# Dilated attention heads of a hybrid decoder layer: the middle statistics travel by DMA through DRAM, and the second stage runs 14 units behind

## The chip, the core and the metric

One core of a Trainium2 chip runs the whole layer in one launch. The metric is the device time of that core in microseconds, the median of three runs.

## The reference, cut to what matters

One input projection gives queries, keys, values and gates for three groups of heads: A (6 heads, banded, with a sink per head), B (6 heads, dilated) and C (4 heads, cross attention to 256 memory tokens). The outputs are gated, joined, projected, normalised and added to the input. The change is about B, where every head is computed three times, with strides 1, 4 and 16, and the three results are weighted by their softmax denominators:

```python
B_CONFIGS = ((128, 1), (512, 4), (2048, 16))
...
        for (win, dil) in B_CONFIGS:
            qs = to_strided(qb * scale, dil)[:, :, :, None, :]
            o, lse = banded_attention(qs, to_strided(kb, dil), to_strided(vb, dil),
                                      win // dil, None)
            outs.append(from_strided(o[:, :, :, 0], B, dil).astype(jnp.float32))
            lses.append(from_strided(lse[..., 0], B, dil))
        wts = jax.nn.softmax(jnp.stack(lses, axis=0), axis=0)
        ob = jnp.sum(wts[..., None] * jnp.stack(outs, axis=0), axis=0)
```

## The kernel before, in words

Three stages follow each other: the projection (to about 1045 us of the profiled execution), attention (to about 1770 us), and the output projection. The change touches attention alone.

**Units, pairs, phases.** Attention of a head runs over two halves of the sequence, so B has 12 phases (head, half), and so has A; C has 8. A unit is 128 queries against 128 or 256 keys. A phase of B has 48 units in 24 pairs: 16 far units (stride 16, pairs 0 to 7), then 8 middle units (stride 4, pairs 8 to 11), 8 near units (stride 1, pairs 12 to 15), 8 middle units (16 to 19) and 8 near units (20 to 23). The first half's far units have 128 keys, the second half's 256. A phase of A has 8 pairs.

**Two stages per pair.** The first stage: TensorE multiplies queries and keys into one of three PSUM places (`scores`, L1311 to L1355), VectorE adds the mask, takes the row's extreme value and writes to SBUF (L1455), ScalarE takes the exponential and its row sum (L1621). The second stage: VectorE multiplies by the unit's weight (`scale`, L1544), TensorE transposes (L1424), ScalarE copies the transpose to SBUF (L1645, L1648), TensorE multiplies with the values (L1408) into one of two banks; VectorE and ScalarE empty a bank after its last pair (L1575, L1609, L1658).

**The exchange.** A row of a far unit, of a middle unit and of a near unit stands for three different tokens, so before the weights can be computed the extremes and sums of the far and the middle units must be brought to the rows of the near units, and the weights must be brought back. Both ways go over TensorE: VectorE spreads 16 far columns with a 0/1 matrix into `moved` (L1489, L1523), TensorE multiplies that by a fixed matrix (L1362, L1369); for the middle ones TensorE multiplies by four fixed 128 x 128 matrices, `group4` (L1364 there, L1371 back), and VectorE picks the right quarter and sums (L1494, L1497 there, L1528, L1532 back). Between the two, VectorE and ScalarE do some small operations on 16 to 48 columns (L1501 to L1519, L1634). The result `coef` is what `scale` waits for.

**The order of the work** is written out by hand, in rounds and slots. A round of B has 24 slots. In slot i each engine handles pair i of the first stage of the newest phase (a), one pair of the second stage of an older phase (c or b), and pieces of the exchange of phase c, the one before a. `TAIL` says how many slots the second stage of a phase starts after the round of its first stage ended: 18. In the round after its first stage, a phase has its exchange in slots 1 to 14: VectorE L1489 at slot 1, TensorE L1362 and L1364 at slot 4, VectorE at slots 5 and 6, ScalarE L1634 at slot 7, VectorE at 9 and 10, TensorE L1369 and L1371 at slot 13, VectorE L1528 to L1532 at slot 14. VectorE scales three slots ahead of the transposes, so from slot 15. Where B gives way to A, the first round of A has 24 slots and the second 22; in the first 11 slots of each there is only second-stage work of B, and A's 8 pairs are spread over the rest:

```python
            lag = (b or c).g.TAIL
            keep = c.g.TAIL if a else 0
            n = lag + c.g.NP - keep
```

**Queues.** SyncE issues all loads and stores of attention in one written order, each behind waits on counters of the first or the second stage. GpSimd's queue issues nothing while B runs: its last DMAs of the projection stage load the first keys and the constants (L984 to L990, among them `sel`, which holds `group4`), and its next one waits for the tenth phase of A (L1919). The fourth PSUM place of the scores, `ps_x`, is the exchange's while B runs; A uses it for scores, so A's fourth pair waits for B's last `coef_ready` (L1344). In A, VectorE copies the head's two sink values to `sink_now` at the first slot of each phase and waits for its own copy (L1447 to L1449).

## Time and profile before

| | before |
|---|---|
| runs, us | 2152.70, 2151.43, 2144.21 |
| median | 2151.43 |
| profiled execution, own time | 2152.24 |
| its span | 2150.1 |
| mean granted TensorE clock | 0.973 |
| busy share of the span: TensorE, VectorE, ScalarE, GpSimd | 95%, 73%, 63%, 5% |

The span goes from the first to the last instruction of the profiled execution; its own time is 2.1 us longer, and 0.8 us above the median. Busy shares are over the whole span, in which B's attention is about a fifth; what limits B must be read in its own stretch. TensorE's busy time is modelled and includes matmuls in flight.

### The profile page before, as it was taken

How to read it: one execution, taken by the hardware profiler on the slowest of the kernel's cores; microseconds unless marked ns; L12 is line 12 of the kernel's file. 1: busy time of each engine (PE TensorE's matmuls, PEld its weight loads, DVE VectorE, ACT ScalarE, POOL GpSimd, SP SyncE). 2: the span in 40 equal slices, each digit the busy share in tenths (PEclk: the TensorE clock that was granted, in tenths of full speed). 3: DMA queues.
4: the chain of work that ended last, by engine and by line, in shares of the span. 5: the costliest groups of instructions: out<-in, count | busy, mean ns of one | idle time of the engine just before them, and what ended most of it. 6: DMA issues, size and time to landing. Idle time of an engine off the chain costs nothing. (4 is left out here: it accounts for less than half of the span.)

```text
span 2150.1 us, 39340 instructions
## 1 busy us (share of the span) xinstructions
PE 2040.4 (95%) x12892; PEld 1717.2 (80%) x12892; DVE 1559.2 (73%) x4410; ACT 1352.9 (63%) x3520; POOL 115.9 (5%) x116
## 2 busy tenths in 40 slices
PE   5999999999999999999889999999999998899998
PEld 4787778888888888888778888887888887688886
DVE  6564674546654574436589999989799997888886
ACT  7454454544555464343699999989699997533333
POOL 1232310000000000002100000000000000000000
PEclk7999999999999999999889999999999999999999
DMA  4466576777577667588876687686779895345543
GB/s 158 152 229 222 177 242 180 217 247 217 155 223 212 225 196 235 184 286 272 201 148 138 130 167 143 131 161 139 150 184 220 227 249 171 98 164 168 176 160 113
DMA packets 351736, 401.40 MB, mean 187 GB/s; under 512 B 105616, under 2 KB 255248, under 8 KB 346688
## 3 DMA queue, kind: packets, MB, share of 16 engines
q1 hardware_dynamic: 343120, 364.80, 62.0%
q0 software_dynamic: 8432, 34.30, 5.2%
q8 instruction: 97, 1.59, 0.3%
q14 instruction: 87, 0.71, 0.1%
HBM read 255.62 MB, written 143.39 MB: 186 GB/s over the span
## 5 line engine op out<-in xcount | busy, mean ns | idle before, releaser
L854 PE MATMUL p_ps<-p_u_hi,p_w_hi 128*128 128x512 f32 x1344 | 534.0, 397 | 26.7 <-DVE p_p_c L739 10.8
L856 PE MATMUL p_ps<-p_u_hi,p_w_lo 128*128 128x512 f32 x1344 | 526.6, 392 | 0.0
L855 PE MATMUL p_ps<-p_u_lo,p_w_hi 128*128 128x512 f32 x1344 | 525.6, 391 | 0.0
L570 DVE TENSOR_TENSOR p_w_lo<-p_w_raw,p_w_hi 128x512 fp32r<-128x512 f32 x336 | 246.6, 734 | 327.0 <-ACT p_w_hi L423 325.4
L1621 ACT ACTIVATE probs<-probs,a_stat 128x256 f32<-128x256 f32 (+1 forms) x896 | 437.4, 497 | 38.9 <-DVE a_stat L1455 36.5
L423 ACT ACTIVATE p_w_hi<-p_w_raw 128x512 fp32r<-128x512 f32 x336 | 211.2, 629 | 329.0 <-PE p_ps L856 304.7
L854 PEld LDWEIGHTS p_ps<-p_u_hi,p_w_hi 128*128 128x128 f32 x1344 | 254.2, 189 | 85.4 <-issue 13.0
L856 PEld LDWEIGHTS p_ps<-p_u_hi,p_w_lo 128*128 128x128 f32 x1344 | 253.7, 189 | 54.4
L855 PEld LDWEIGHTS p_ps<-p_u_lo,p_w_hi 128*128 128x128 f32 x1344 | 254.2, 189 | 50.8
L1455 DVE CUSTOM_DVE_ANT_0 probs<-a_ps_s,fixed 128x256 f32<-128x256 f32 (+1 forms) x704 | 251.9, 398 | 48.3 <-PE a_ps_s L1354 45.7
L1424 PE MATMUL a_ps_t<-fixed,probs 128*128 128x128 f32 x1660 | 262.0, 279 | 23.6 <-ACT a_pT L1645 16.5
L1544 DVE TENSOR_SCALAR probs<-probs,a_coef 128x256 f32<-128x256 f32 (+1 forms) x896 | 264.5, 341 | 3.0
L1645 ACT ACTIVATE a_pT<-a_ps_t 128x512 f32<-128x512 f32 (+1 forms) x412 | 232.8, 568 | 20.7 <-PE a_ps_t L1424 20.6
L1408 PE MATMUL a_ps_o<-a_pT,a_v 128*64 128x128 f32 x3320 | 238.4, 283 | 0.0
L1353 PE MATMUL a_ps_s<-k_hi,q 128*128 128x256 f32 (+1 forms) x672 | 216.4, 341 | 15.4 <-PEq L266 5.8
L1424 PEld LDWEIGHTS a_ps_t<-fixed,probs 128*128 128x128 f32 x1660 | 194.8, 143 | 39.5 <-DVE probs L1544 23.3
L1408 PEld LDWEIGHTS a_ps_o<-a_pT,a_v 128*64 128x64 f32 x3320 | 183.4, 138 | 36.8 <-issue 34.4
L1354 PE MATMUL a_ps_s<-k_lo,q 128*128 128x256 f32 (+1 forms) x672 | 191.1, 301 | 0.0
L1621 ACT ACTIVATION_READ_ACCUMULATOR probs<-probs,a_stat 128x1 f32 x896 | 182.0, 203 | 0.0
L1353 PEld LDWEIGHTS a_ps_s<-k_hi,q 128*128 128x128 f32 x672 | 136.6, 203 | 44.7 <-issue 32.8
L2225 PE MATMUL f_ps<-f_w_hi,parts_hi 128*128 128x512 f32 x368 | 144.4, 392 | 6.5 <-DVE probs L2141 4.1
L2226 PE MATMUL f_ps<-f_w_lo,parts_hi 128*128 128x512 f32 x384 | 150.1, 391 | 0.0
(202 smaller groups left out, 2762.6 us busy)
## 6 DMA issues: line engine op xcount, KB each, us to landing
p_w_raw<-in_w_in SPq DMA_DIRECT2D x156, 256.0 KB, 3.7
p_w_raw<-scratch_w_s SPq DMA_DIRECT2D x144, 256.0 KB, 3.6
scratch_qk_hi<-p_out_a SPq DMA_DIRECT2D x80, 256.0 KB, 4.0
scratch_qk_lo<-p_out_b SPq DMA_DIRECT2D x80, 256.0 KB, 4.1
a_v<-scratch_v SPq DMA_DIRECT2D x40, 512.0 KB, 8.2
scratch_gate<-p_out_a SPq DMA_DIRECT2D x64, 256.0 KB, 3.8
scratch_v<-p_out_a SPq DMA_DIRECT2D x256, 64.0 KB, 2.3
a_gate<-scratch_gate SPq DMA_DIRECT2D x64, 256.0 KB, 6.0
```

Source lines behind the costliest of these rows:

```text
L423: nc.scalar.activation(w_hi[:, m % 3, :, :], w_raw[:, entry(j, g), :, :], ACT.Copy).then_inc(w_hi_ready, 1)
L570: nc.vector.tensor_tensor(w_lo[:, m % 3, :, :], w_raw[:, entry(j, g), :, :], w_hi[:, m % 3, :, :].bitcast(F32), ALU.subtract).then_inc(w_l ...
L854: nc.tensor.matmul(bank, hi, u_hi[j][:, k, :], start=j < 2 and k == 0, stop=False, skip_group_check=True)
L855: nc.tensor.matmul(bank, hi, u_lo[j][:, k, :], start=False, stop=False, skip_group_check=True)
L856: last = nc.tensor.matmul(bank, lo, u_hi[j][:, k, :], start=False, stop=k == KH - 1, skip_group_check=True)
L1353: nc.tensor.matmul(out, w, keys_of(keys_hi, u), start=True, stop=False)
L1408: last = nc.tensor.matmul(place_of(ps_o[j * HD:(j + 1) * HD, bank % 2, :], u), v[name][:, half, tile, :], pT[:, e % 4, j, at * P:(at + 1) ...
L1424: last = nc.tensor.transpose(ps_t[:, e % 2, j, at * P:(at + 1) * P], probs[:, s, 2 * e + j, at * P:(at + 1) * P], ident[:])
L1455: last = nc.vector.tensor_tensor_reduce(out=probs[:, s, 2 * slot + j, a:], in0=ps_s[:, slot % NS, j, a:], in1=masks[u.kind][:, a:], scale= ...
L1544: last = nc.vector.tensor_scalar(place, place, coef[:, s, u.column:u.column + 1], None, ALU.mult)
L1621: last = nc.scalar.activation(place, place, ACT.Exp, scale=-1.0, bias=stat[:, s, 0, u.column:u.column + 1], accum_out=stat[:, s, 1, u.colu ...
L1645: nc.scalar.activation(pT[:, e % 4, :, a[0]:], ps_t[:, e % 2, :, a[0]:], ACT.Copy).then_inc(turned_copied, 1)
```

## The change

The way of the middle statistics and weights is taken from TensorE and VectorE and given to DMAs on GpSimd's queue. When 20 of the 24 pairs of a phase have their sums, GpSimd stores 32 columns of `stat` to a DRAM scratch, waits, and issues four loads that bring them back in the new arrangement; VectorE waits for them at slot 2 of the next round. When the weights are ready (slot 5), GpSimd stores 16 columns, waits and issues four loads into `coef`; VectorE waits for them before pair 8's `scale`. `group4`, `picked` and the picking operations go; three operations on two of the groups at once become two operations each. The far statistics are spread at slot 9 of the phase's own round, right after their pairs, and multiplied at slot 11; the far weights at slots 5 and 7. The other operations of the exchange move to slots 1 to 9, at three places inside a slot, with other work between dependent ones. `TAIL` becomes 14. In A the copy of the sinks goes, and the operands are read from the table itself.

```diff
-    TAIL = 18 if kind == "B" else 4
+    TAIL = 14 if kind == "B" else 4
...
-        def exchange(phase, slot):
-            p, s = number(phase), phase[1]
-            if kind == "B" and slot == 4:
-                pe.wait_ge(spread, p + 1)
+        def gather(phase, slot):
+            if kind == "B" and slot == 11:
+                pe.wait_ge(spread, number(phase) + 1)
                 for x in range(2):
-                    nc.tensor.matmul(ps_x[:, 16 * x:16 * x + 16], moved[:, x, :], col16, start=True, stop=True)
-                for b in range(NCH):
-                    last = nc.tensor.matmul(ps_x[:, 128 + 32 * b:160 + 32 * b].rearrange("p (x n) -> p x n", x=2), group4[:, b, :],
-                                            stat[:, s, :, 16:32], start=True, stop=True)
+                    last = nc.tensor.matmul(ps_x[:, 16 * x:16 * x + 16], moved[:, x, :], col16, start=True, stop=True)
                 last.then_inc(gathered, 1)
-            if kind == "B" and slot == 13:
-                pe.wait_ge(spread_back, p + 1)
-                nc.tensor.matmul(ps_x[:, 64:80], moved[:, 2, :], col16, start=True, stop=True)
-                for r in range(NCH):
-                    last = nc.tensor.matmul(ps_x[:, 256 + 16 * r:272 + 16 * r], group4[:, r, :], work[:, 7, 16:32],
-                                            start=True, stop=True)
-                last.then_inc(gathered_back, 1)
+
+        def give_back(phase, slot):
+            if kind == "B" and slot == 7:
+                pe.wait_ge(spread_back, number(phase) + 1)
+                nc.tensor.matmul(ps_x[:, 64:80], moved[:, 2, :], col16, start=True, stop=True).then_inc(gathered_back, 1)
...
-            if kind == "A" and slot == 0:
-                dve.nop(nofuse=True)
-                nc.vector.tensor_copy(sink_now[:, s, :], sink[:, :, bass.ds(h, 1)].rearrange(
-                    "p a o -> p (a o)")).then_inc(sink_ready, 1)
-                dve.wait_ge(sink_ready, p + 1)
-                start = sink_now[:, s, 1:2] if kind == "A" else 3e38
+                start = sink[:, 1, h:h + 1] if kind == "A" else 3e38
...
-        def inverse(phase, slot):
+        def inverse(phase, slot, place):
 
             p, s = number(phase), phase[1]
-            if slot == 1:
+            if (slot, place) == (1, 0):
                 dve.wait_ge(sums_ready, p * NP + NP)
                 if kind == "A":
                     dve.wait_ge(exps_ready, p + 1)
-                    nc.vector.tensor_tensor(work[:, 1, :], work[:, 0, :], stat[:, s, 1, :],
-                                            ALU.add).then_inc(step, 1)
+                    nc.vector.tensor_tensor(work[:, 1, :], work[:, 0, :], near_stat(s, 1), ALU.add).then_inc(step, 1)
                     dve.wait_ge(step, p + 1)
-                    nc.vector.reciprocal(coef[:, s, :], work[:, 1, :]).then_inc(coef_ready, 1)
-                else:
-                    nc.vector.reciprocal(coef[:, s, :], stat[:, s, 1, :]).then_inc(coef_ready, 1)
-
-        def exchange(phase, slot):
+                nc.vector.reciprocal(coef[:, s, :], work[:, 1, :] if kind == "A" else near_stat(s, 1)).then_inc(coef_ready, 1)
+
...
+        def exchange(phase, slot, place):
...
-            if slot == 1:
+            at = (slot, place)
+            done = p * DVE_STEPS
+            far = ps_x[:, 0:32].rearrange("p (x b) -> p x b", x=2)
+            middle = middles.rearrange("p (b x c) -> p x c b", x=2, c=NCH)
+            by_chunk = lambda of: of.rearrange("p (c b) -> p c b", b=NCH)
+            low, ex, inv = work[:, 1, 0:16], work[:, 3, :], work[:, 6, 0:16]
+            if at == (1, 2):
+                dve.wait_ge(max_ready, p * NP + NP)
+                dve.wait_ge(gathered, p + 1)
+                nc.vector.tensor_tensor(work[:, 0, 0:16], far[:, 0, :], near_stat(s, 0), ALU.min).then_inc(step, 1)
+            if at == (2, 0):
+                dve.wait_ge(step, done + 1)
+                dve.wait_ge(middle_loaded, 64 * p + 64)
+                nc.vector.tensor_tensor(by_chunk(low), middle[:, 0, :, :], by_chunk(work[:, 0, 0:16]), ALU.min).then_inc(step, 1)
+            if at == (2, 1):
+                dve.wait_ge(step, done + 2)
+                nc.vector.tensor_tensor(work[:, 2, 0:16], low, far[:, 0, :], ALU.subtract)
+                nc.vector.tensor_tensor(by_chunk(work[:, 2, 16:32]), by_chunk(low), middle[:, 0, :, :], ALU.subtract)
+                nc.vector.tensor_tensor(work[:, 2, 32:48], low, near_stat(s, 0), ALU.subtract).then_inc(shifted, 1)
+            if at == (4, 0):
+                dve.wait_ge(exps_ready, p + 1)
                 dve.wait_ge(sums_ready, p * NP + NP)
-                nc.vector.tensor_tensor(moved[:, 0:2, :].rearrange("p x (r a) -> p x r a", a=8),
-                                        stat[:, s, :, 0:16].unsqueeze(3).broadcast_to([P, 2, 16, 8]),
-                                        sel16.unsqueeze(1).unsqueeze(1).broadcast_to([P, 2, 16, 8]), ALU.mult).then_inc(spread, 1)
...
+                nc.vector.tensor_tensor(work[:, 4, 0:16], ex[:, 0:16], far[:, 1, :], ALU.mult)
+                nc.vector.tensor_tensor(by_chunk(work[:, 4, 16:32]), by_chunk(ex[:, 16:32]), middle[:, 1, :, :], ALU.mult)
+                nc.vector.tensor_tensor(work[:, 4, 32:48], ex[:, 32:48], near_stat(s, 1), ALU.mult).then_inc(step, 1)
+            if at == (4, 1):
+                dve.wait_ge(step, done + 3)
+                nc.vector.reduce_sum(work[:, 5, 0:16], work[:, 4, :].rearrange("p (a n) -> p n a", a=3),
+                                     mybir.AxisListType.X).then_inc(step, 1)
+            if at == (4, 2):
+                dve.wait_ge(step, done + 4)
+                nc.vector.reciprocal(inv, work[:, 5, 0:16]).then_inc(step, 1)
+            if at == (5, 0):
+                dve.wait_ge(step, done + 5)
+                nc.vector.tensor_tensor(work[:, 7, 0:16], ex[:, 0:16], inv, ALU.mult)
+                nc.vector.tensor_tensor(work[:, 7, 16:32].rearrange("p (b c) -> p c b", c=NCH), by_chunk(ex[:, 16:32]),
+                                        by_chunk(inv), ALU.mult).then_inc(weights_ready, 1)
...
+            if at == (5, 1):
+                dve.wait_ge(weights_ready, p + 1)
                 nc.vector.tensor_tensor(moved[:, 2, :].rearrange("p (n a) -> p n a", a=8),
                                         work[:, 7, 0:16].unsqueeze(2).broadcast_to([P, 16, 8]),
                                         sel16.unsqueeze(1).broadcast_to([P, 16, 8]), ALU.mult).then_inc(spread_back, 1)
-            if slot == 14:
+            if at == (9, 0):
                 dve.wait_ge(gathered_back, p + 1)
-                own(nc.vector.tensor_tensor(picked[:, 0:64].rearrange("p (n b) -> p n b", b=NCH),
-                                            ps_x[:, 256:320].rearrange("p (n b) -> p n b", b=NCH),
-                                            col4.unsqueeze(1).broadcast_to([P, 16, NCH]), ALU.mult))
-                nc.vector.tensor_copy(coef[:, s, 0:16], ps_x[:, 64:80])
-                nc.vector.reduce_sum(coef[:, s, 16:32].rearrange("p (c r) -> p r c", r=NCH),
-                                     picked[:, 0:64].rearrange("p (r c b) -> p r c b", r=NCH, b=NCH),
-                                     mybir.AxisListType.X).then_inc(coef_ready, 1)
+                nc.vector.tensor_copy(coef[:, s, 0:16], ps_x[:, 64:80]).then_inc(coef_ready, 1)
...
+        def spread_far(phase, slot):
+
+            if kind != "B" or slot != 9:
+                return
+            p, s = number(phase), phase[1]
+            dve.wait_ge(sums_ready, p * NP + 8)
+            nc.vector.tensor_tensor(moved[:, 0:2, :].rearrange("p x (r a) -> p x r a", a=8),
+                                    stat[:, s, 0:32].rearrange("p (x r) -> p x r", x=2).unsqueeze(3).broadcast_to([P, 2, 16, 8]),
+                                    sel16.unsqueeze(1).unsqueeze(1).broadcast_to([P, 2, 16, 8]), ALU.mult).then_inc(spread, 1)
...
                 dve.wait_ge(coef_ready, p + 1 + C1)
+            if kind == "B" and e == 8:
+                dve.wait_ge(middle_back, 64 * p + 64)
...
-            if kind == "B" and slot == 7:
-                act.wait_ge(shifted, 2 * p + 1)
+                nc.scalar.activation(work[:, 0, :], near_stat(s, 0), ACT.Exp,
+                                     bias=sink[:, 0, phase[0]:phase[0] + 1]).then_inc(exps_ready, 1)
+            if kind == "B" and slot == 3:
+                act.wait_ge(shifted, p + 1)
                 nc.scalar.activation(work[:, 3, :], work[:, 2, :], ACT.Exp).then_inc(exps_ready, 1)
...
+    def pool_parts(pool):
+
+        def gather(phase):
+
+            p, s = number(phase), phase[1]
+            pool.wait_ge(sums_ready, p * NP + 20)
+            pool.dma_start(sc["middle_stats"], stat[:, s, 32:64]).then_inc(middle_stored, 16)
+            pool.wait_ge(middle_stored, 32 * p + 16)
+            for b in range(NCH):
+                pool.dma_start(middles[:, 8 * b:8 * b + 8],
+                               sc["middle_stats"][32 * b:32 * b + 32, :].rearrange("j (r e) -> r j e", r=NCH)).then_inc(middle_loaded, 16)
+
+        def give_back(phase):
+
+            p, s = number(phase), phase[1]
+            pool.wait_ge(weights_ready, p + 1)
+            pool.dma_start(sc["middle_weights"], work[:, 7, 16:32]).then_inc(middle_stored, 16)
+            pool.wait_ge(middle_stored, 32 * p + 32)
+            for r in range(NCH):
+                pool.dma_start(coef[:, s, 16 + 4 * r:20 + 4 * r],
+                               sc["middle_weights"][32 * r:32 * r + 32, :].rearrange("j (b c) -> b j c", c=NCH)).then_inc(middle_back, 16)
+        return named(gather=gather, give_back=give_back)
...
-                    c.parts.exchange(c.phase, i)
+                    c.parts.give_back(c.phase, i)
+                for v in slot.new:
+                    a.parts.gather(a.phase, v)
                 if slot.two_before and slot.two_before[1] % 2:
                     for x, e in (slot.three_before, slot.two_before):
                         x.parts.times_values(x.phase, e)
...
-                if c and c.g.kind != "B":
-                    c.parts.exchange(c.phase, i)
+                if c:
+                    c.parts.exchange(c.phase, i, 0)
                 if slot.ahead:
                     x, e = slot.ahead
                     x.parts.scale(x.phase, e)
+                if c:
+                    c.parts.exchange(c.phase, i, 1)
                 for v in slot.new:
                     a.parts.scores(a.phase, v)
...
-                if c and c.g.kind == "B":
-                    c.parts.exchange(c.phase, i)
+                if c:
+                    c.parts.exchange(c.phase, i, 2)
+                for v in slot.new:
+                    a.parts.spread_far(a.phase, v)
...
+        def pool_round(a, c, b, d):
+            if c and c.g.kind == "B":
+                c.parts.give_back(c.phase)
+            if a and a.g.kind == "B":
+                a.parts.gather(a.phase)
...
+                rounds(pool, pool_round, lambda g: g.pool_parts(pool))
...
+        "middle_stats": scratch("middle_stats", [P, 32]), "middle_weights": scratch("middle_weights", [P, 16]),
...
-    sel = np.concatenate([j % 8 == n(8), j // 8 == n(16), j // 32 == n(4)]
-                         + [j == 32 * b + n(P) % 32 for b in range(NCH)], 1).astype(np.float32)
+    sel = np.concatenate([j % 8 == n(8), j // 8 == n(16)], 1).astype(np.float32)
```

## Rows read from the trace of the kernel before

**Rows 1.** Windows: three of B's ten full rounds and the sum of all ten; busy us, clock, DMA share

```profile
1139.78:1179.56 39.78, 37.07 (x367) 32.25 (x366) 37.37 (x176) 37.15 (x127) 0.00 (x0) 1.00 0.80 154
...
1258.77:1299.85 41.08, 41.08 (x389) 36.70 (x390) 36.81 (x178) 37.46 (x134) 0.00 (x0) 0.94 0.69 135
...
1339.64:1378.97 39.33, 38.70 (x386) 34.34 (x385) 36.68 (x176) 36.78 (x134) 0.00 (x0) 1.00 0.69 140
...
sum 399.70, PE 383.35 PEld 337.04 DVE 370.44 ACT 371.31 POOL 0.00; mean PE 38.33 PEld 33.70 DVE 37.04 ACT 37.13 POOL 0.00
```

**Rows 2.** Waits in the ten full rounds, 1100.04 to 1499.74: total, times, longest

```profile
ACT probs L1621 <- DVE a_stat L1455: 22.4, 45, 0.9
DVE probs L1455 <- PE a_ps_s L1354: 21.6, 43, 1.7
PE a_ps_t L1424 <- ACT a_pT L1645: 11.1, 25, 1.8
...
ACT a_pT L1645 <- PE a_ps_t L1424: 4.7, 10, 0.6
```

**Rows 3.** TensorE's middle exchange: its instructions, and the way back in the timeline

```profile
L1364 PE MATMUL a_ps_s<-a_stat,fixed x96: 276/276/401, 1071.4 to 1505.4; 128*128 128x32 f32 x96
...
1118.17 1.04 PE L1371 MATMUL a_ps_s<-a_work,fixed 128*128 128x16 f32 x8
```

**Rows 4.** Lines of the exchange on VectorE: duration ns min/median/max, first and last start

```profile
L1494 DVE TENSOR_TENSOR a_picked<-a_ps_s,fixed x12: 285/288/292, 1074.2 to 1505.9; 128x128 f32<-128x128 f32 x12
...
L1497 DVE TENSOR_REDUCE a_ps_s<-a_picked x12: 294/295/295, 1074.5 to 1506.2; 128x32 f32<-128x128 f32 x12
...
L1528 DVE TENSOR_TENSOR a_picked<-a_ps_s,fixed x12: 217/218/220, 1087.3 to 1521.8; 128x64 f32<-128x64 f32 x12
...
L1532 DVE TENSOR_REDUCE a_coef<-a_picked x12: 209/209/213, 1087.7 to 1522.1; 128x16 f32<-128x64 f32 x12
...
L1489 DVE TENSOR_TENSOR a_moved<-a_stat,fixed x12: 420/423/428, 1070.4 to 1499.7; 128x256 f32<-128x256 f32 x12
...
L1510 DVE TENSOR_TENSOR a_work<-a_work,a_ps_s x12: 182/186/190, 1079.1 to 1510.0; 128x32 f32<-128x32 f32 x12
```

**Rows 5.** ScalarE's timeline around slots 13 and 14 of one round

```profile
1200.53 0.60 ACT L1645 ACTIVATE a_pT<-a_ps_t 128x512 f32<-128x512 f32 x1 [0.63 <-PE a_ps_t L1424]
...
1203.57 0.51 ACT L1621 ACTIVATE probs<-probs,a_stat 128x256 f32<-128x256 f32 x1 [0.83 <-DVE a_stat L1455]
```

**Rows 6.** Timeline at the change from B to A

```profile
1505.86 0.29 DVE L1494 TENSOR_TENSOR a_picked<-a_ps_s,fixed 128x128 f32<-128x128 f32 x1 [3.40 <-PE a_ps_s L1364]
...
1522.40 0.39 PE L1353 MATMUL a_ps_s<-k_hi,q 128*128 128x256 f32 x1 [1.98 <-DVE a_coef L1532]
...
1541.36 1.09 PE L1408 MATMUL a_ps_o<-a_pT,a_v 128*64 128x128 f32 x16
...
1543.41 1.09 PE L1408 MATMUL a_ps_o<-a_pT,a_v 128*64 128x128 f32 x16
```

**Rows 7.** Windows: the eleven slots without scores in A's first round; six phases of A

```profile
1499.74:1513.41 13.67, 13.51 (x89) 11.21 (x90) 8.74 (x37) 6.66 (x20) 0.00 (x0) 0.63 0.86 176
1566.90:1649.20 82.30, 79.25 (x772) 68.08 (x769) 80.82 (x339) 79.02 (x262) 0.00 (x0) 1.00 0.90 212
```

**Rows 8.** VectorE's timeline at the first slot of a phase of A

```profile
1582.06 0.18 DVE L1447 COPY a_sink_now<-fixed 128x2 f32<-128x2 f32 x1
1582.39 0.48 DVE L1455 CUSTOM_DVE_ANT_0 probs<-a_ps_s,fixed,a_sink_now 128x256 f32<-128x256 f32 x1
```

**Rows 9.** DMA issues (KB each, median us to landing), and one issue in GpSimd's timeline

```profile
scratch_v<-p_out_a SPq DMA_DIRECT2D x256, 64.0 KB, 2.3
...
p_spare<-in_x POOLq DMA_DIRECT2D x24, 512.0 KB, 4.5
...
381.39 0.53 POOL L932 DMA_DIRECT2D p_spare<-in_x  x1 [19.40 <-PE p_ps_t L826]
```

**Rows 10.** Timeline: the 20th pair's sum, and VectorE's end of slot 1 in the next round

```profile
1172.03 0.20 ACT L1621 ACTIVATION_READ_ACCUMULATOR probs<-probs,a_stat 128x1 f32 x1
...
1179.56 0.42 DVE L1489 TENSOR_TENSOR a_moved<-a_stat,fixed 128x256 f32<-128x256 f32 x1
```

85 lines of the change are left out of this document (26 added, 59 removed).

## The prediction

> **What bounds the kernel now.** I read the stretch of B alone, cut into its full rounds, first by busy time and then by waits. In ten full rounds (399.7 us) ScalarE is busy 371.3 us and VectorE 370.4; TensorE's 383.4 includes matmuls in flight [rows 1]. So a round of 39 to 41 us has three engines with 93% or more of work, and what is to be gained is what the fullest one still waits. The waits say who waits for whom: ScalarE loses 22.4 us to VectorE's row extremes and 4.7 us to TensorE's transposes, 27.1 of its 28.4 idle us; VectorE loses 21.6 us to TensorE's scores, and TensorE 11.1 us to ScalarE's copies [rows 2]. It is a ring with small buffers, and ScalarE is its fullest member. Without any idle time of ScalarE a round would take 37.1 us instead of 40.0; that 2.8 us per round is the ceiling of everything the change can do in full rounds, as long as no work leaves ScalarE, and none does. In two of the ten rounds (41.08 us, clock 0.94) TensorE is busy throughout, since part of the round was granted the lower clock of 1.2 GHz; there TensorE is the bound [rows 1].
>
> **The full rounds (ten).** Removed on TensorE: eight instructions there and eight back per phase (96 in 12 phases); eight take 1.04 us, so 2.1 us per round [rows 3]. Removed on VectorE: 0.29 + 0.29 at slot 5, 0.22 + 0.21 at slot 14, 1.01 us in all. Added: three operations that did two groups become two each; next to each other such small ones (0.19 us) overlap to about 0.1, so +0.3 [rows 4]. Net 0.7 us of VectorE. What of it lies on the path is read from ScalarE's idle places:
> - Slot 13: TensorE's block of eight stands before a transpose for which ScalarE waits 0.63 us [rows 5]; over the ten rounds these waits are 4.7 us [rows 2], so 0.47 per round. All go.
> - Slot 14: behind the picks ScalarE waits 0.83 us for VectorE [rows 5]. 0.43 of that is the picks. They go; the rest is the bank's emptying, which stays and only moves.
> - Slots 4 to 6: TensorE's other block and the 0.58 us of picks. VectorE waits there for scores, but ScalarE has its copies of queries in the same slots, and no idle place of it lies there in an undisturbed round. This I cost at nothing: the cover is ScalarE's own work, and if it were gone up to 0.9 us per round would come on top.
> - Given back: the 0.42 us of L1489 moves from slot 1 to slot 9, where with the shorter lag a bank is emptied as well. Half of it, 0.2, I put on the path.
> - In the two rounds on the lower clock TensorE is the bound, and the rest of its 2.1 us counts: 1.2 us twice, 0.2 per round as a mean.
>
> 0.47 + 0.43 - 0.2 + 0.2 = 0.9 us per round, **-9 us**. Bounds: 0 (the idle time only changes its place) and -1.8 (nearly TensorE's whole 2.1).
>
> **The first exchange**, in B's second round, is mostly without second-stage work: **-1** (0 to -2).
>
> **The last exchange**, in A's first round. Its first eleven slots run at a mean clock of 0.63 [rows 7], so TensorE's first block costs nearly double, 1.9 us, and VectorE stands 3.40 us for it; later TensorE stands 1.98 us until the weights are ready, because A's fourth pair needs `ps_x` [rows 6]. With the exchange done at slot 9 and that pair at slot 13, this wait has no cause left. 1.9 + 1.0 + 1.98 = 4.9, of which TensorE will wait for something else in part: **-4** (-1 to -5).
>
> **The shorter lag.** Four slots go, from A's second round (22 to 18). Four pairs' second stage leave the stretch in which there is nothing else to do. There two pairs take 1543.41 - 1541.36 = 2.05 us [rows 6], so four 4.1 us. They turn up in B's second round, beside scores, where ScalarE gets four more copies: 0.60 us is one of 512 columns [rows 5]; those of the first half's far units are half as large, I take 0.4 each, 1.6 us. **-2.5** (0 to -5). SyncE's queue is in written order; loads of values and stores of results wait for the second stage and come free four slots earlier, loads of keys and queries wait for scores and don't move. Nothing on it gets later.
>
> **Group A.** From the sink copy to the first score operation it is 0.33 us [rows 8]. In six phases VectorE is busy 80.8 of 82.3 us [rows 7], so it is the bound and the copy is on the path; ScalarE at 79.0 is next. Ten phases by 0.25: **-2.5** (0 to -4). Group C issues the same work: nothing.
>
> **The constants.** `sel` shrinks by 516 of 540 columns, 264 KB. It is loaded before attention starts; at the 135 to 154 GB/s that the full rounds move [rows 1] that would be up to 2 us. I take 0, since other constants are queued with it (0 to -2).
>
> **The added waits.** Each round VectorE waits at slot 2 for the four loads, with its whole queue behind it: the `scale` and the scores of slot 2, and through these TensorE and ScalarE. The time given: 1172.23 (the twentieth pair's sum) to 1179.98 (the end of L1489, the end of slot 1), 7.75 us [rows 10]; the bank's emptying leaves these slots, so 7.0 to 7.75. The time needed is a store, its landing, four issues (three more by 0.53, 1.6 us) and a landing. No small transfer on GpSimd's queue stands alone in the trace. From below: SyncE's 64 KB store, 2.3 us; from above: GpSimd's 512 KB load, 4.5 us [rows 9]. The chain is then 2.3 + 1.6 + 2.3 = 6.2 to 4.5 + 1.6 + 4.5 = 10.6 us. It is nearer the small one in size and the other in queue; the bytes are 16 KB and less, so I take 2.8, the chain 7.2, and 0.3 us late in 12 phases: **+3.6** (0 to the rival below). The way back has 14 slots from the ready weights to pair 8's `scale`, some 20 us, three times the chain: nothing, and it would cost only if a landing took 9 us. GpSimd's own queue has nothing else while B runs; the waits of the one phase's return stand before the next phase's store and are over ten slots before it.
>
> The Trainium skill, "DMA: Bandwidth & Descriptors", section "Anatomy of one DMA", gives some 2.0 us per transfer of this queue whatever its size. By that figure, an estimate, the chain is 5.6 us, this term is 0 and the sum 3.6 us lower; no run here shows it yet.
>
> **The sum**: -9 - 1 - 4 - 2.5 - 2.5 + 3.6 = -15.4. The profiled execution took 2152.24 us, so 2136.8; its own time is 0.8 us above the median. I predict **2137 us**. A measurement of this kernel can tell about 0.5% from no change, here 10.8 us: faster means below 2140.7.
>
> **Rivals.**
> - *The loads come late* (slower). Place: VectorE at slot 2, in 12 rounds. If the landings take 4.5 us the chain is 2.8 us later than its 7.75 us. ScalarE has about 1.2 us of work in hand, so 1.6 us per round are lost, 18 us in eleven rounds; TensorE runs dry meanwhile, and eight rounds that now keep the full clock would cost like those that don't, 41.08 - 39.33 = 1.75 us [rows 1], 14 us more. Against the other terms' -19: +13, **2165 us**. It decides when a landing passes about 3.5 us; the change loses outright from about 4.3. For it: SyncE's transfers move 135 to 154 GB/s in the same rounds. Against: the DMA share of these rounds is 0.69 to 0.80, so there is room [rows 1]. 17 in 100. The Trainium skill, same page, section "Rules for kernel authors", says that the slowest dimension of both patterns sets how many DMA engines share a transfer; each load's source begins with a dimension of 4, so it would run on 4 of 16, which speaks for this rival. No row of before shows it.
> - *The idle time only moves.* ScalarE bounds the rounds, the denser slots 8 to 10 of VectorE take back what slots 13 and 14 gave: full rounds 0, the rest -6.4: **2146 us**. For it: VectorE is as full as ScalarE. 25 in 100.
> - *TensorE is the true bound.* Its 2.1 us count nearly whole: -18 for the full rounds, chain hidden: **2124 us**. For it: VectorE's 21.6 us of waiting for scores. Against: TensorE itself waits 11.1 us for ScalarE [rows 2]. 15 in 100.
> - *My forecast*, 2129 to 2141: 43 in 100.
>
> **How the numbers follow.** Below 2140.7 lie the forecast but for its last corner, and the third rival: 0.57. Within 0.5%: the second rival and small delays: 0.26. Slower: 0.17. The range must leave out no more than 2 in 10: from 2121 (all favourable bounds but one) to 2165 (the late loads at the upper row).
>
> **What would show it.** Right: no L1364 or L1371, ten full rounds of 38.5 to 39 us, ScalarE's waits for transposes near 0, its waits for VectorE about 20 us and moved to slots 8 to 10 and 16 to 18; the first operation of slot 2 starts without a wait for a DMA of over 0.5 us; GpSimd's loads land in under 3 us. The stretch from B's last scores to A's third phase is 6 us shorter. Wrong: a line in the waits in which VectorE stands for `middles`, longer than 1 us and in every round; the granted clock down in most rounds; or full rounds still near 39.9.

## The result: slower by 1.7%, and the profile after

The changed kernel takes 2184.52 us (median; 2178.78 to 2191.07, four runs), the kernel before, measured beside it, 2148.57 (2144.21 to 2152.70): ratio **1.0169**, with a 95% interval of [1.013, 1.0207]. 2137 was forecast, with a range up to 2165. The profiled execution took 2186.16 us; its span is 2184.3 us against 2150.1 before.

I cut both spans at the same five places: VectorE's first score operation of B's first, third and twelfth phase, and ScalarE's exponential of A's third and twelfth phase. Windows of the kernel before:

```profile
1047.00:1098.70 51.70, 44.03 (x246) 39.67 (x245) 40.66 (x233) 49.53 (x200) 0.00 (x0) 0.75 0.72 134
1098.70:1458.30 359.60, 347.27 (x3378) 305.70 (x3377) 332.81 (x1575) 333.89 (x1170) 0.00 (x0) 0.98 0.73 143
1458.30:1582.80 124.50, 114.64 (x1108) 98.11 (x1106) 105.15 (x439) 98.15 (x303) 0.00 (x0) 0.95 0.70 145
1582.80:1702.06 119.26, 115.74 (x1137) 100.09 (x1136) 117.26 (x495) 117.31 (x393) 1.07 (x2) 1.00 0.92 221
1702.06:2150.10 448.04, 420.33 (x2517) 351.33 (x2515) 370.61 (x868) 236.15 (x631) 3.35 (x5) 0.98 0.54 167
```

and of the changed one (columns as in [rows 1]: length, then busy time of TensorE, weight loads, VectorE, ScalarE and GpSimd, clock, DMA share, GB/s):

```profile
1047.10:1105.00 57.90, 46.55 (x260) 41.94 (x260) 42.55 (x242) 51.41 (x207) 7.68 (x12) 0.69 0.69 124
1105.00:1498.30 393.30, 349.67 (x3247) 297.95 (x3246) 323.75 (x1566) 334.58 (x1168) 62.02 (x94) 0.95 0.71 133
1498.30:1612.04 113.74, 103.12 (x1033) 86.52 (x1031) 99.70 (x423) 95.34 (x299) 10.57 (x16) 1.00 0.80 156
1612.04:1731.13 119.09, 114.49 (x1127) 99.07 (x1126) 115.42 (x482) 117.12 (x393) 1.14 (x2) 1.00 0.92 219
1731.13:2184.30 453.17, 424.33 (x2526) 354.70 (x2524) 371.17 (x870) 236.53 (x631) 3.35 (x5) 0.97 0.54 166
```

Nine of B's rounds cost 33.7 us more, the stretch with the first exchange 6.2 more; the passage from B to A costs 10.8 us **less**, A the same, and the remainder 5.1 more. VectorE is busy 9 us less in the nine rounds (323.75 against 332.81; 0.7 per round was forecast), and ScalarE as long as before; so they wait. Single rounds of the changed kernel:

```profile
1154.50:1194.50 40.00, 36.20 (x343) 30.05 (x342) 36.48 (x175) 36.84 (x127) 5.68 (x10) 1.00 0.82 164
1194.50:1242.00 47.50, 40.90 (x379) 35.52 (x378) 35.53 (x174) 37.54 (x134) 7.73 (x12) 0.93 0.62 110
1242.00:1281.90 39.90, 36.55 (x346) 30.36 (x344) 36.53 (x175) 37.19 (x129) 5.96 (x10) 1.00 0.83 167
1281.90:1328.30 46.40, 39.73 (x375) 34.36 (x375) 35.60 (x174) 37.08 (x133) 7.25 (x11) 0.93 0.63 111
```

They alternate: over the nine rounds, those of a head's second half take 39.3 to 40.0 us and those of a first half 45.5 to 49.5. The waits of the nine rounds (1105.0 to 1498.3; against [rows 2]) name what is new:

```profile
ACT probs L1620 <- DVE a_stat L1455: 53.2, 51, 6.4
DVE a_work L1489 <- DMA a_middles<-scratch_middle_stats: 47.5, 9, 8.6
PE a_ps_s L1364 <- DVE a_stat L1455: 22.8, 9, 5.3
DVE probs L1455 <- PE a_ps_s L1365: 18.7, 28, 2.9
```

VectorE stands at slot 2 in each of the nine rounds, and behind it ScalarE (53.2 us of waiting for VectorE, 20.1 in the same nine rounds before) and TensorE. Four of the waits one by one in VectorE's timeline:

```profile
1204.59 0.18 DVE L1489 TENSOR_TENSOR a_work<-a_middles,a_work 128x16 f32<-128x16 f32 x1 [8.51 <-DMA a_middles<-scratch_middle_stats]
1246.12 0.18 DVE L1489 TENSOR_TENSOR a_work<-a_middles,a_work 128x16 f32<-128x16 f32 x1 [2.02 <-DMA a_middles<-scratch_middle_stats]
1291.73 0.18 DVE L1489 TENSOR_TENSOR a_work<-a_middles,a_work 128x16 f32<-128x16 f32 x1 [8.29 <-DMA a_middles<-scratch_middle_stats]
1332.36 0.18 DVE L1489 TENSOR_TENSOR a_work<-a_middles,a_work 128x16 f32<-128x16 f32 x1 [1.94 <-DMA a_middles<-scratch_middle_stats]
```

What distinguishes the first two stands in the timelines of GpSimd and of SyncE's queue:

```profile
1190.72 0.59 POOL L1682 DMA_DIRECT2D scratch_middle_stats<-a_stat  x1 [19.25 <-ACT probs L1620]
1192.73 2.75 POOL L1685 DMA_DIRECT2D a_middles<-scratch_middle_stats  x4 [1.42 <-DMA scratch_middle_stats<-a_stat]
...
1191.93 1.34 SPq L1246 DMA_DIRECT2D k_hi<-scratch_qk_hi  x2
1193.32 3.50 SPq L1246 DMA_DIRECT2D k_lo<-scratch_qk_lo  x2
1196.87 10.85 SPq L1262 DMA_DIRECT2D a_v<-scratch_v  x2
...
1237.23 0.59 POOL L1682 DMA_DIRECT2D scratch_middle_stats<-a_stat  x1 [21.51 <-ACT probs L1620]
1239.25 2.74 POOL L1685 DMA_DIRECT2D a_middles<-scratch_middle_stats  x4 [1.43 <-DMA scratch_middle_stats<-a_stat]
...
1241.21 1.95 SPq L1262 DMA_DIRECT2D a_v<-scratch_v  x2
```

Just before the 47.5 us round SyncE issues four 512 KB loads, the keys of the next head's second half, in the very microseconds in which GpSimd issues its four loads of 4 KB, and from 1196.87 two loads of values behind them; the last of the small loads has landed only at 1204.59. In the other round SyncE has two value loads there, issued later. The share of the DMA engines that is busy, in 40 slices (each digit is tenths), from 1190 to 1205 and from 1236 to 1251:

```profile
DMA  9787010004569999999999999999999999999999
DMA  9999701000005051658999999999992799897100
```

In the first the engines are full from about 1194.5 on, while the small loads are still being issued; in the second most of the 3 us in which they are issued (1239.25 to 1241.99) is quiet. The issues of the whole run (KB each, median us to landing), with the minimum, median and maximum of the 48 small loads:

```profile
k_lo<-scratch_qk_lo SPq DMA_DIRECT2D x24, 512.0 KB, 10.6
a_middles<-scratch_middle_stats POOLq DMA_DIRECT2D x48, 4.0 KB, 4.6
scratch_middle_stats<-a_stat POOLq DMA_DIRECT2D x12, 16.0 KB, 1.7
...
L1685 POOL DMA_DIRECT2D a_middles<-scratch_middle_stats x48: 677/682/949, 1072.7 to 1540.0; - x48
DMA to landing us min/median/max: 2.1/4.6/9.8
```

A small load lands in 2.1 to 9.8 us after its issue. An issue keeps GpSimd 0.68 us, not the 0.53 of [rows 9].

### The profile page after: what moved, and what is told of

The parts are those of the page before. It is cut to its first block, busy times and chain, and to the rows that moved or that the text cites. A ratio compares the mean times of both kernels' runs of the same rounds, so it can differ in the third digit from the quotient of the medians.

```text
span 2184.3 us, 39076 instructions
## 1 busy us (share of the span) xinstructions
PE 2036.4 (93%) x12700; PEld 1702.8 (78%) x12700; DVE 1546.2 (71%) x4386; ACT 1352.7 (62%) x3520; POOL 196.4 (9%) x236
## 4 chain that ended last, share of the span: by engine, by line
PE 28%; DVE 8%; DMA 6%; ACT 5%; issue 3%; POOL 1%; SPq 1%; DVEq 0%; ACTq 0%
PE a_ps_o L1413 5%; PE f_ps L2259 4%; PE f_ps L2260 4%; PE f_ps L2261 4%; PE a_ps_t L1429 4%; ACT probs L1620 3%; PE a_ps_s L1364 3%; DMA a_middles<-scratch_middle_stats 3%; PE a_ps_s L1365 2%; DVE probs L1455 2%; DVE probs L1543 2%; DMA scratch_middle_stats<-a_stat 1%; DMA scratch_y<-a_gate 1%; POOL a_middles L1685 1%; ACT a_pT L1644 1%
## 5 line engine op out<-in xcount | busy, mean ns | idle before, releaser
L1455 DVE CUSTOM_DVE_ANT_0 probs<-a_ps_s,fixed 128x256 f32<-128x256 f32 (+1 forms) x896 | 336.1, 414 | 49.0 <-PE a_ps_s L1365 47.2
L1364 PE MATMUL a_ps_s<-k_hi,q 128*128 128x256 f32 (+1 forms) x672 | 220.0, 345 | 39.2 <-DVE a_stat L1455 32.3
L1620 ACT ACTIVATION_READ_ACCUMULATOR probs<-probs,a_stat 128x1 f32 x896 | 175.4, 196 | 0.0
```

Source lines behind the costliest of these rows:

```text
L1364: nc.tensor.matmul(out, w, keys_of(keys_hi, u), start=True, stop=False)
L1455: last = nc.vector.tensor_tensor_reduce(out=probs[:, s, 2 * slot + j, a:], in0=ps_s[:, slot % NS, j, a:], in1=masks[u.kind][:, a:], scale= ...
L1620: last = nc.scalar.activation(place, place, ACT.Exp, scale=-1.0, bias=stat_of(s, 0, u), accum_out=stat_of(s, 1, u))
```

## The experiments

Ratios are against the kernel before, measured on the same chip; for spans of stretches I use the profiled executions. Edits are to the changed kernel unless said otherwise.

**1. Keys behind the middles.** The load of keys in `loads` (L1246) waits for the middles' landing when it is for a head's second half. SyncE's queue is in written order, so the loads of values behind the keys wait too:

```diff
+                if s:
+                    sp.wait_ge(middle_loaded, 128 * h)
```

> The changed kernel, but SyncE waits for the four loads of the middle statistics before it issues the key loads of a head's second half. Theory (the key loads are in the way): in the changed kernel VectorE stands about 8.5 us for the loads in every second round, in which keys are loaded at the same time, and 2 us in the others. Here the long waits become 2 to 3 us, the total falls from 60.8 to 25 to 35 us, and the time from 2184 to 2150 to 2165 us. Rival (the four loads are slow by themselves, because each runs on few DMA engines or the queue is slow): the long waits stay above 6 us, the time stays within 5 us of 2184.

Measured: 2146.05 us, ratio **0.9952** [0.993, 0.9974]. One edit on SyncE's queue turns 1.7% slower into 0.5% faster, further than expected. The nine rounds take 353.7 us (393.3), the long ones are gone; 15.2 us of waiting for middles are left in them. The same waits (L1491 here) and the landings:

```profile
1185.96 0.18 DVE L1491 TENSOR_TENSOR a_work<-a_middles,a_work 128x16 f32<-128x16 f32 x1 [1.07 <-DMA a_middles<-scratch_middle_stats]
1226.62 0.18 DVE L1491 TENSOR_TENSOR a_work<-a_middles,a_work 128x16 f32<-128x16 f32 x1 [2.10 <-DMA a_middles<-scratch_middle_stats]
...
DMA to landing us min/median/max: 2.0/2.1/4.8
```

**2. The exchange two slots later.** Middle statistics used in slot 4, weights ready in slot 7, everything behind them two to three slots later:

```diff
-            if at == (2, 0):
+            if at == (4, 0):
...
-            if at == (5, 0):
+            if at == (7, 0):
```

> The changed kernel with the whole exchange two slots later (the wait for the middle loads at slot 4 instead of 2, the weights at slot 11 instead of 9, the far gather at slot 14 instead of 11); same work, same lag of 14. Theory (only the lateness costs): two slots are about 3 us, so the short waits go and the long ones become 5 to 6 us, in total 25 to 32 us instead of 60.8, and the time 2150 to 2160 us. Rival (the place of the other operations, or the DMAs as such, costs): waits shrink as said but the time stays above 2170.

Measured: 2160.84 us, ratio **1.0034** [1.001, 1.0057]. VectorE waits for middles 29.3 us in 7 of B's 12 exchanges (60.8 in 12 in the changed kernel), but the rounds beside the keys still take 42 to 44 us: there the loads land later than two slots make good. 373.9 us for the nine rounds.

**3. Both edits.**

> Both edits. If late loads are all that is wrong with the change, VectorE waits less than 0.5 us per round for them, and what is left is what the prediction gave the rest of the change, -19 us against before: about 2130 us, 2122 to 2138. If the saved work of TensorE and VectorE is worth nothing, only the last exchange, the lag and group A count: about 2140. If DMAs or the new places cost something themselves: at or above 2149.

Measured: 2146.3 us, ratio **0.9951** [0.9933, 0.9968]. The middles are waited for in two rounds only (9.0 us), yet it is no faster than experiment 1 and 16 us above what was expected: VectorE now waits 13.9 us in 11 places for ScalarE's small exponential, which stands in ScalarE's queue at slot 5.

**4. The lag alone, back to 18.**

```diff
-    TAIL = 14 if kind == "B" else 4
+    TAIL = 18 if kind == "B" else 4
```

> The changed kernel with the lag back at 18 instead of 14, all else as changed. The prediction gave the lag 2.5 us (0 to 5): 2187 us against the changed kernel's 2184, with the same waits for the middle loads. If the shorter lag itself causes the long waits (value loads that come free earlier and fall on the middle loads), the waits fall by over 15 us and the time with them, below 2170.

Measured: 2192.95 us, ratio **1.0176** [1.0133, 1.022]. The passage from B to A takes 119.6 us instead of 113.7, and the nine rounds 405.9 instead of 393.3, at a mean clock of 0.89 instead of 0.95; long waits for middles stay (49.3 us in 8 exchanges, 60.8 in 12 before the edit). The shorter lag is not what makes the change slow.

**5. Group A's copy alone.** The kernel **before**, with the copy of the sinks left out and the sinks read in place, as in the change.

```diff
...
-                start = sink_now[:, s, 1:2] if kind == "A" else 3e38
+                start = sink[:, 1, h:h + 1] if kind == "A" else 3e38
...
```

> The kernel before with nothing changed but group A's copy of the sinks gone: the prediction put this at -2.5 us (0 to -4), ratio 0.9988. If VectorE is not A's bound, 1.000. In the trace a phase of A should take 0.25 us less of its 13.3 us.

Measured: 2153.78 us, ratio **0.9987** [0.9962, 1.0013]. The interval is wider than the 2.5 us in question, but the trace decides: from A's third to its twelfth phase it is 119.4 us against 119.3, so the copy cost nothing. B is untouched here, and yet its nine rounds took 365.4 us in this profiled execution against 359.6 in the other: two rounds ran 43.7 us at a clock of 0.85. So nine rounds of one profile of this kernel are known to no better than 6 us.

**6. The kernel before without its way for the middle units.** TensorE's `group4` matmuls and VectorE's picks left out, old order, lag 18; the middle units use their own rows' statistics and weights.

```diff
-                for b in range(NCH):
-                    last = nc.tensor.matmul(ps_x[:, 128 + 32 * b:160 + 32 * b].rearrange("p (x n) -> p x n", x=2), group4[:, b, :],
-                                            stat[:, s, :, 16:32], start=True, stop=True)
...
```

> The kernel before with the middle way left out: no multiplications by group4, no picks; the middle units use their own rows' statistics and weights (that part of the computation is wrong), in the old order and with the lag of 18, no DMA in its place. Same small operations as in the changed kernel. The prediction gave this -9 us in the ten full rounds, -1 and -2.9 in the first and last exchange: about -13, ratio 0.994, full rounds of 38.7 to 39.1 us instead of a mean of 39.97. Rival (the idle time only moves): full rounds within 0.2 us of before, -1 to -4 us in all.

Measured: 2150.8 us, ratio **0.9973** [0.995, 0.9996]; the nine rounds take 359.2 us, like before. Rounds at the full clock are 0.4 to 0.7 us shorter than before, but two run partly on the lower clock (0.86 and 0.85), at 42.2 and 43.0 us, and take it back. The passage takes 121.8 us, 2.7 less. Taking the work away, in the old order, gives little in this stretch as a whole.

**7. The changed kernel without its transfers.** GpSimd's round, the waits for it and the trip of the weights are gone; the rows' own values take the place of the spread ones.

```diff
-            middle = middles.rearrange("p (b x c) -> p x c b", x=2, c=NCH)
+            middle = stat[:, s, 32:64].rearrange("p (b x c) -> p x c b", x=2, c=NCH)
...
-                rounds(pool, pool_round, lambda g: g.pool_parts(pool))
```

> The changed kernel with none of its DMAs and none of the waits for them: the middle units use their own rows' statistics and weights (that part of the computation is wrong); all else as changed: new places, lag 14, sinks. It is the change at a price of nothing for the DMAs. The prediction's other terms give -19 us against before: 2130 to 2136, ratio 0.991. If the saved work is worth nothing and only the last exchange, the lag and A count: -9, ratio 0.996, full rounds of 39.3 to 39.9. If it is not faster than the kernel with the key loads moved (ratio 0.9952), the short waits of 2 us per round that are left there cost nothing.

Measured: 2131.98 us, ratio **0.9894** [0.9859, 0.993]. Nine rounds: 351.8 us. Without waits and transfers the change would be 1.1% faster, about 23 us; the interval, 15 to 30 us, also holds the 19 that the forecast gave without the waits.

**8. Every transfer issued, but nobody waits at slot 2.** This separates the transfers from the wait; at slot 2 VectorE takes the rows' own values.

```diff
-            middle = middles.rearrange("p (b x c) -> p x c b", x=2, c=NCH)
+            middle = stat[:, s, 32:64].rearrange("p (b x c) -> p x c b", x=2, c=NCH)
...
-                dve.wait_ge(middle_loaded, 64 * p + 64)
...
             if at == (9, 0):
+                dve.wait_ge(middle_loaded, 64 * p + 64)
```

> The changed kernel with every transfer of GpSimd's queue still issued where it was, but VectorE's second slot takes the rows' own statistics instead of the spread ones, so that it waits for no transfer there; the wait for the loads stands seven slots later (slot 9), where they have long landed. The weights still go through memory and back. Theory (only the wait in slot 2 costs): the six rounds beside the key loads fall from 46 to 39 us, VectorE waits for middles under 1 us in all, and the time is that of the kernel without the transfers, 2132 us, ratio 0.987 to 0.991. Rival (the 12 x 10 small transfers cost by being there, beside the key loads or on GpSimd's queue): full rounds of 40 us or more, ratio 0.995 or above. Second rival (the way back of the weights is late too): a new wait at the scaling of unit pair 8, over 10 us in all.

Measured: 2136.63 us, ratio **0.9908** [0.9875, 0.9942]. The landings are as late as in the changed kernel, and it does not matter:

```profile
DMA to landing us min/median/max: 2.0/4.6/10.1
...
1047.90:1101.20 53.30, 44.67 (x260) 39.84 (x259) 42.34 (x241) 51.76 (x208) 7.48 (x12) 0.76 0.75 138
1101.20:1452.50 351.30, 333.91 (x3249) 285.63 (x3247) 323.77 (x1567) 331.18 (x1166) 62.27 (x94) 1.00 0.81 149
1452.50:1564.67 112.17, 102.76 (x1032) 86.37 (x1030) 100.18 (x423) 94.91 (x298) 10.27 (x16) 1.00 0.80 158
```

The nine rounds take 351.3 us, with the small transfers and the key loads side by side. So what the transfers cost by their presence is the 0.14% between experiments 7 and 8, less than either interval, and nothing in the nine rounds; the wait is the loss. Of the 49.5 us by which the span of the changed kernel is longer than this one's, 42.0 are in the nine rounds, beside 47.5 us of waits. The two kinds of wait have two prices: the four of 1.8 to 2.5 us, 8.3 us together, lengthen their rounds by 1.9 us against experiment 8, and the five of 6.8 to 8.6 us, 39.2 together, theirs by 40.2. A short wait is mostly covered by work in hand, a long one is lost whole. Experiment 1 agrees: the 15.2 us of waits left there, none above 3.3, cost 2.4 us (353.7 against 351.3).

**9. The lag without the waits.** Experiment 7 with `TAIL = 18`, to price the lag where nothing covers it.

> The kernel without the transfers (own rows' statistics and weights, the changed order) with the second stage 18 units behind instead of 14: the lag alone, where no wait for a transfer covers it. The prediction priced the shorter lag at 2.5 us. Theory: the stretch from B's last phase to A's third exchange grows from 110.7 us to 116 to 118 (as 113.7 grew to 119.6 when the changed kernel was given the lag of 18), so the time rises by about 6 us, to 2138 us, ratio 0.992 to 0.994. Rival (a longer lag gives the full rounds more slack and wins back what it loses at the end): ratio 0.988 to 0.990, with the full rounds at 38.5 us or less.

Measured: 2141.29 us, ratio **0.9938** [0.9914, 0.9962]: the lag is worth 9.3 us between the medians (not measured side by side), not 2.5. Between the profiled executions it is 9.7. The passage grows by 6.7 us (117.4 against 110.7), and, which I had not expected, the nine rounds by 4.6 (356.4 against 351.8); the remainder is 1.5 us shorter. Three rounds:

```profile
1180.80:1221.40 40.60, 40.57 (x362) 35.50 (x361) 35.27 (x175) 36.65 (x133) 0.00 (x0) 0.88 0.66 132
1221.40:1261.50 40.10, 36.59 (x364) 31.39 (x364) 36.67 (x175) 37.65 (x128) 0.00 (x0) 1.00 0.79 157
1261.50:1299.80 38.30, 36.52 (x359) 31.90 (x355) 34.90 (x175) 36.03 (x133) 0.00 (x0) 1.00 0.71 140
```

The first and the third are the same kind of round, a head's first half; part of the first was granted 1.2 GHz (a mean of 0.88), TensorE is busy throughout, and it takes 2.3 us longer. Two of the nine rounds are so. At the full clock the longer lag only shifts time from one kind to the other: a first half takes 38.3 us instead of 39.2, a second half 40.1 instead of 39.0. Had the two slow rounds taken 38.3 as well, the nine would have grown by 0.2 us instead of 4.6.

**10. A version faster than both the kernel before and the changed one: one slot later, keys behind.** Experiment 1, with the middle statistics used in slot 3, the exponential in slot 4 and the rest as in experiment 2.

> The changed kernel with the key loads behind the middle loads, the middle wait one slot later (slot 3), ScalarE's small exponential at slot 4 and its readers two slots after it (slot 6) instead of one, the far gather at slot 14. In the kernel with both edits VectorE stood 1.5 us per round for that exponential. Expected: waits for the middle loads under 1 us per round and none for the exponential, full rounds of 38.9 to 39.3 us, ratio 0.991 to 0.994. If the waits were covered already: as the kernel with the key loads moved, 0.995.

Measured: 2139.14 us, ratio **0.9911** [0.9877, 0.9946]; nine rounds in 350.6 us. VectorE waits for middles 10.9 us in 3 exchanges, most of it in the first exchange; for the exponential 0.5 us.

**11. The same, with the first gate and values held too.** SyncE holds the first head's gate and its v4 and v1 values (`B.gate(h, 0)`, `B.v(h, 0, ["v4", "v1"])`) until the first middles have landed.

```diff
+                    if h == 0:
+                        sp.wait_ge(B.middle_loaded, 64)
                     B.gate(h, 0)
```

> The exchange one slot later with the keys behind the middles, and besides SyncE holds the first head's gate and its v4 and v1 values until the first phase's middles have landed. Theory (in the first exchange the middles land late because 2 MB of values and gate are on the way beside them): the wait of 9.8 us in the first round falls to 5 us or less, the stretch from B's start to its third phase from 57.5 us to about 53, and the time to 2135 us, ratio 0.989 to 0.991 against 0.9911. Rival (the first window is simply too short, its slots take 1 us each): the landing falls but the wait stays above 7 us, and the held values come late to the second stage; ratio 0.991 to 0.994.

Measured: 2134.53 us, ratio **0.9902** [0.9864, 0.9941], the lowest median of those that leave nothing out; against experiment 10 the intervals overlap, so which of the two is faster is not shown. VectorE's waits over B, this kernel:

```profile
DVE a_work L1491 <- DMA a_middles<-scratch_middle_stats: 7.4, 4, 5.4
DVE probs L1545 <- DMA a_coef<-scratch_middle_weights: 3.1, 2, 2.1
```

The first wait fell only from 8.2 to 5.4 us and the stretch up to B's third phase only to 55.3 us. From the issue of the store to the use of the loads it is 7.7 us there (1065.89 to 1073.61), against 6.4 in a quiet round of experiment 1 (1179.54 to 1185.96). So some 4 us of the stall would stand with a quiet chain too: VectorE is at slot 2 only 2.4 us after the store was issued.

| | span of nine rounds | B's twelfth phase to A's third | ratio |
|---|---|---|---|
| before | 359.6 | 124.5 | 1 |
| changed | 393.3 | 113.7 | 1.0169 |
| 1 keys behind | 353.7 | 113.6 | 0.9952 |
| 8 nobody waits | 351.3 | 112.2 | 0.9908 |
| 7 no transfers | 351.8 | 110.7 | 0.9894 |
| 9 no transfers, lag 18 | 356.4 | 117.4 | 0.9938 |
| 11 first loads held too | 349.3 | 111.7 | 0.9902 |

## Why the prediction was wrong

One term made the miss: **the added waits**, "the chain 7.2, and 0.3 us late in 12 phases: +3.6". Experiment 8 has all of the change but the wait at slot 2; it takes 19.6 us less than the kernel before (the interval of its ratio is 12 to 27 us), where the other terms said 19. The wait then costs 47.9 us between the medians (2184.52 - 2136.63, not measured side by side), 49.5 between the spans and about 56 by the two ratios, where 3.6 was put. What made it so large:

- *The landing.* I took 2.8 us between rows of 2.3 and 4.5 and let 4.5 be the upper end. Both are medians over transfers elsewhere. The median landing is 2.1 us in experiment 1, with the keys held back, and 4.6 in the changed kernel, up to 9.8 beside the 512 KB loads. In the round at 1190 the chain runs from the twentieth pair's sum, 1190.44, to 1204.59, 14.2 us, where the upper end was 10.6. In the round at 1237 it is 9.2 us (1236.95 to 1246.12), in a quiet round of experiment 1 6.7 (1179.25 to 1185.96). I did ask whether there was room, and answered with the DMA share of whole rounds, 0.69 to 0.80. The question was what SyncE issues in the 7 us of the chain. The order of its loads would have told: the keys of a head's second half are released by the last scores of the head before (`load_k` waits for `scores_ready`), and the middles of that same phase travel in these very slots. Why a small load lands late beside large ones, and whether the engines, their queues or the memory hold it, isn't shown; the DMA engines are full then.
- *The window.* I read 7.0 to 7.75 us from one round. In the changed kernel it is 7.1 us in every second round (VectorE arrives at 1246.12 - 2.02 = 1244.10) and 5.6 in the others (1204.59 - 8.51 = 1196.08), which begin with the short units of a first half, of 128 keys: the short window and the long landing fall on the same rounds. In the first exchange it is shorter still, and there it is the store that is late: 5.1 us to landing beside loads of values, the four loads behind it 2.1 us.
- *The issues*: 0.68 us each for these loads, 0.53 taken; 0.45 us for three.

The rival *the loads come late* was right in kind. Its threshold, "loses outright from about 4.3", fits the median landing of 4.6, but that is partly luck, since no round has the landing it assumed for all. Its price was 32 us before the other terms, for a landing of 4.5 in every round alike; in fact VectorE stands 6.8 to 8.6 us in one kind of round and 1.8 to 2.5 in the other. The 1.2 us of work in hand that it set against this hold for the short waits (experiment 8), but the long ones have no such cover. So its 2165, the end of the range, was 20 us too low. My 17 in 100 rested on the mean DMA share. The Trainium skill's 2.0 us per transfer ("DMA: Bandwidth & Descriptors", section "Anatomy of one DMA") agrees with the quiet landings of 2.0 to 2.2 us of the 4 KB loads (the 16 KB store's median is 1.7), but a landing beside other traffic is up to 9.8 us here. The Trainium skill's rule on that page that a slowest dimension of 4 leaves 4 of 16 engines ("Rules for kernel authors"), which I had put behind the rival, does not make the loads late by itself: the same patterns have a median of 2.1 us once the keys are held back. Whether it makes them more exposed to the key loads was not tried.

The other terms were right in sum only, and that is luck: by the spans of experiment 8 the full rounds gave -8.3, the first exchange +1.6, the passage -12.3 and group A 0, which adds to the -19 forecast although three of the four terms are off.

- *Full rounds*, -9 in ten. Nine take 8.3 us less in experiment 8 (351.3 against 359.6): the size is right, as far as one profile of before can tell (experiment 5). Its make-up is so in part. ScalarE's waits for transposes, 4.4 us, are gone, as forecast, and VectorE's waits for scores fall from 20.3 to 12.5 us; but ScalarE's waits for VectorE, which were to lose 0.43 per round, only go from 20.1 to 19.2, and a new wait of 12.8 us for ScalarE's small exponential takes part back, which I had not priced. By rounds, the four second halves give 5.2 us together, the three first halves at the full clock 0.2, and the two at a clock of 0.92 before give 2.9, 0.3 per round as a mean where I put 0.2. Over the nine rounds the clock is 1.00 in experiments 1, 7, 8, 10 and 11, 0.98 before.
- *Last exchange and lag*, -4 and -2.5. The passage is 12.3 us shorter in experiment 8 and 10.8 in the changed kernel. By experiment 9 the lag is 6.7 of the passage in a kernel without transfers, and the rest, 124.5 - 117.4 = 7.1, is the exchange: 2.7 for TensorE's and VectorE's work (experiment 6, where I had 1.9 + 1.0) and 4.4 for its new order and places, where I had 1.98. Both were sized too low, the lag beyond its bound of 5. I counted the second stage's work of four pairs. 4.3 of the 6.7 stand between B's last score operation and A's first: 13.2 us at a clock of 0.74 with the lag of 18, 8.9 us at 1.00 with 14; 1.3 stand in B's last round and 1.1 behind.
- *First exchange*, -1. The stretch is +1.6 with nobody waiting, +6.2 with the wait: wrong sign. Of the 1.6 only 0.3 stand in the second round, where the exchange is (33.1 us against 32.8), and 1.2 in the first, which has none; why the first is longer was not tried. With the wait the second round takes 37.5 us: it has almost no second stage, so no cover, and its window is the shortest of all.
- *Group A*, -2.5. Zero (experiment 5). That VectorE is busy 80.8 of 82.3 us showed that it is the fullest, not that 0.25 us in its first slot cannot be made up within the phase.
- *Constants*, 0: B begins at 1047 in both. Among all the profiled executions it begins between 1041.7 and 1048.8, so the 2 us of the bound could not be seen.
- *The way back of the weights*, 0: right, although its landings too come late in experiment 8.

Open: the remainder behind A's twelfth phase differs by up to 10 us between profiled executions (444.6 in experiment 5, 454.3 in experiment 10), with no edit there, and it is in every ratio as noise. Why it varies wasn't tried. The kernel before varies more as a whole: beside experiment 8 its seventeen runs go from 2139.82 us, at a mean clock of 0.977, to 2165.72 at 0.968, while experiment 8's seven lie between 2134.16 and 2140.00. So a part of what the change gives without its wait may be rounds that keep the full clock more reliably; it was not separated from the work saved.

## What to carry to other kernels

A wait for a small transfer is priced by what the other queues issue in the same microseconds, not by a median landing or the mean DMA share of a round: list the large loads that the same event releases, and read the window and the DMA engines' load in these very microseconds for each kind of round. If a chain through memory must be short, hold the bulk loads behind it; that one wait on SyncE's queue was worth 40 us of the span here (2184.3 against 2144.1). And price a shorter pipeline lag in two places: the stretch at the end in which work stands beside nothing, and the rounds between, where the granted clock can change with it.

## What the runs showed of the hardware

- A 4 KB load issued by GpSimd mostly lands in 2.0 to 2.2 us when SyncE's key loads are held back (experiments 1 and 10), but in up to 9.8 us when four 512 KB loads of SyncE's queue are issued in the same 5 us and two more behind them, and that at a mean DMA share of 0.62 in that round.
- The large loads hardly suffered in return: k_lo's median landing is 10.6 us in the changed kernel, 10.1 with the keys behind the middles.
- TensorE's granted clock was lower with the longer lag in both pairs of kernels that differ in the lag alone: over the nine rounds 0.97 with 18 and 1.00 with 14 without transfers (experiments 9 and 7), 0.89 and 0.95 with them (experiment 4 and the changed kernel). Each is one profiled execution, and why was not tried.
